# Router products by channel quarter, top-2 ranks from the logits, and five banks for the last expert's additions

## The reference, cut to what matters

```python
def moe_swiglu(h, w_router, e_gate, e_up, e_down):
    probs = jax.nn.softmax(jnp.einsum('btd,de->bte', h, w_router).astype(jnp.float32), axis=-1)
    top_v, top_i = lax.top_k(probs, TOP_K)
    top_v = top_v / jnp.sum(top_v, -1, keepdims=True)
    combine = jnp.sum(jax.nn.one_hot(top_i, N_EXPERTS, dtype=jnp.float32) * top_v[..., None], axis=-2)
    y = jnp.zeros_like(h)
    for e in range(N_EXPERTS):
        y = y + combine[..., e:e + 1].astype(h.dtype) * swiglu(h, e_gate[e], e_up[e], e_down[e])
    return y
```

## Time and profile before

| | |
|---|---|
| time, median of 3 runs | 1687.37 us (1682.82 to 1691.30) |
| the profiled execution | 1686.86 us, its span 1685.1 us |
| busy: PE, PEld | 1566.8 us (93%), 1343.1 us (80%) |
| busy: DVE, ACT, POOL | 1183.6 us (70%), 902.6 us (54%), 41.1 us (2%) |
| from HBM | 406.75 MB, 245 GB/s over the span |
| issued weight loads of the experts | 268 of 1024 KB |

### The profile page before, as it was taken

One profiled execution on the slowest core, in us unless ns is written; L12 is line 12 of the kernel. 1 busy time (PEld: TensorE's weight loads), 2 busy tenths in 40 slices (PEclk: granted clock), 3 DMA queues, 4 the chain that ended last, 5 costly groups with the idle time before them and its releaser, 6 DMA issues.

```text
span 1685.1 us, 23549 instructions
## 1 busy us (share of the span) xinstructions
PE 1566.8 (93%) x9218; PEld 1343.1 (80%) x9218; DVE 1183.6 (70%) x1232; ACT 902.6 (54%) x822; POOL 41.1 (2%) x76
## 2 busy tenths in 40 slices
PE   6999988799999799886799999999999999999995
PEld 3778777699999699775778888888888888888873
DVE  2332447755556865666598988889788888988875
ACT  2544423433333456242377767677676766767653
POOL 2100010000000010000000000000000000000000
PEclk9899978999999899878699999999999999999997
DMA  9999844254444252231299999999999999999990
GB/s 315 326 338 313 281 139 127 80 158 150 149 148 146 75 171 99 60 107 51 75 326 361 359 309 354 335 363 350 309 358 339 364 340 319 357 341 365 331 333 32
DMA packets 242035, 415.10 MB, mean 246 GB/s; under 512 B 7891, under 2 KB 128893, under 8 KB 241926
## 3 DMA queue, kind: packets, MB, share of 16 engines
q1 hardware_dynamic: 238662, 402.31, 69.7%
q0 software_dynamic: 3264, 11.28, 2.3%
HBM read 406.75 MB, written 6.82 MB: 245 GB/s over the span
## 4 chain that ended last, share of the span: by engine, by line
PE 54%; DVE 4%; ACT 1%; issue 1%; DVEq 0%; ACTq 0%
PE bank L608 15%; PE bank L610 15%; PE bank L609 15%; PE bank L1035 1%; PE bank L997 1%; PE bank L611 1%; PE bank L612 1%; PE bank L613 1%; PE bank L1077 1%; PE bank L712 1%; PE bank L727 1%; PE bank L1078 1%; PE bank L952 1%; PE bank L731 0%; PE bank L963 0%
## 5 line engine op out<-in xcount | busy, mean ns | idle before, releaser
L1496 DVE TENSOR_TENSOR w_lo<-raw_ring,w_hi 128x2048 fp32r<-128x2048 f32 x264 | 604.5, 2291 | 110.9 <-ACT w_hi L1234 110.1
L1234 ACT ACTIVATE w_hi<-raw_ring 128x2048 fp32r<-128x2048 f32 x264 | 506.7, 1919 | 238.5 <-PE bank L610 238.5
L608 PE MATMUL bank<-w_hi,xg_hi 128*128 128x512 f32 (+1 forms) x768 | 294.1, 383 | 5.4 <-DVE xg_lo L1986 5.4
L610 PE MATMUL bank<-w_hi,xg_lo 128*128 128x512 f32 (+1 forms) x768 | 289.8, 377 | 0.0
L609 PE MATMUL bank<-w_lo,xg_hi 128*128 128x512 f32 (+1 forms) x768 | 289.5, 377 | 0.0
L611 PE MATMUL bank<-act_hi,w_hi 128*128 128x320 f32 x736 | 240.4, 327 | 33.2 <-DVE act_lo L1546 20.3
L612 PE MATMUL bank<-act_lo,w_hi 128*128 128x320 f32 x736 | 234.7, 319 | 0.0
L613 PE MATMUL bank<-act_hi,w_lo 128*128 128x320 f32 x736 | 234.3, 318 | 0.0
L1487 DVE TENSOR_TENSOR w_lo<-raw_ring,w_hi 128x2048 fp32r<-128x2048 f32 x65 | 148.7, 2288 | 103.0 <-ACT w_hi L1174 102.8
L611 PEld LDWEIGHTS bank<-act_hi,w_hi 128*128 128x128 f32 x736 | 145.6, 198 | 39.3 <-issue 30.6
L608 PEld LDWEIGHTS bank<-w_hi,xg_hi 128*128 128x128 f32 x768 | 145.2, 189 | 30.5 <-DVE xg_lo L1986 5.6
(11 more groups left out here) (311 smaller groups left out, 2000.7 us busy)
## 6 DMA issues: line engine op xcount, KB each, us to landing
raw_ring<-in_e_gate_dram SPq DMA_DIRECT2D x90, 1024.0 KB, 5.2
raw_ring<-in_e_up_dram SPq DMA_DIRECT2D x90, 1024.0 KB, 5.3
raw_ring<-in_e_down_dram SPq DMA_DIRECT2D x88, 1024.0 KB, 5.0
raw_ring<-in_w_ada_dram SPq DMA_DIRECT2D x24, 1024.0 KB, 7.7
raw_ring<-in_w_in_dram SPq DMA_DIRECT2D x24, 1024.0 KB, 7.6
st<-in_w_ada_dram SPq DMA_DIRECT2D x12, 1024.0 KB, 8.5
kdsp<-in_w_ada_dram SPq DMA_DIRECT2D x12, 1024.0 KB, 9.6
raw_ring<-in_w_ff_gate_dram SPq DMA_DIRECT2D x11, 1024.0 KB, 5.4
```

The source lines that it names most:

```text
L608: pe.matmul(out, xh, wh, start=start, stop=False)
L610: return pe.matmul(out, xl, wh, start=False, stop=stop)
L1234: act.activation(w_hi[:, (NSPLIT + i) % SPL, :], raw[:, s, :], ACT.Copy).then_inc(hi_ready.sem, 1)
L1496: dve.tensor_tensor(w_lo[:, r, :], raw[:, s, :], w_hi[:, r, :].bitcast(F32), ALU.subtract).then_inc(lo_ready.sem, 1)
```

## The change

- The router's products are made by channel quarter: TensorE waits for quarter a of `hf` and multiplies its two channel slices for all token tiles, then waits for the next. The three tiles' sums now stand open side by side, in banks 5, 6 and 7, and DVE copies them with three instructions.
- The comparisons that give the ranks read the logits (`lg[:, 0]`) and not the probabilities. The sum, the reciprocal and the product that make the probabilities move behind the second token turn, in front of the routing weights; ACT's Exp stays where it is.
- The position counts (`places`) stand between the third and the fourth token turn on TensorE, and DVE's work on them between the fourth and the fifth.
- The last expert's scatter goes through banks 0 to 4 in turn; only the sixth to eighth wait for a bank to be read. The other experts' scatters stay on bank 0.

```diff
--- before.py
+++ after.py
@@ -943,15 +943,30 @@
                         sums(l, 1, m)
 
 
-            pe.wait_ge(hp_ready.sem, hp_ready.at(DEPTH - 1, 7))
-            pe.wait_ge(hs_ready.sem, hs_ready.at(DEPTH - 1, 7))
             rows_of = [[(0, P, 0)], [(0, P, P)], [(0, TS, TP), (TS, P, TP)]]
-            for t in range(NT):
-                for kk in range(KD):
-                    for r0, r1, t0 in rows_of[t]:
-                        last = pe.matmul(bank[5][r0:r1, t * NE:(t + 1) * NE], hf[:, kk, t0:t0 + r1 - r0], w_rt[:, kk, :],
-                                         start=(kk == 0), stop=(kk == KD - 1))
+            for a in range(4):
+                pe.wait_ge(hp_ready.sem, hp_ready.at(DEPTH - 1, 4 + a))
+                pe.wait_ge(hs_ready.sem, hs_ready.at(DEPTH - 1, 4 + a))
+                for kk in (2 * a, 2 * a + 1):
+                    for t in range(NT):
+                        for r0, r1, t0 in rows_of[t]:
+                            last = pe.matmul(bank[5 + t][r0:r1, 0:NE], hf[:, kk, t0:t0 + r1 - r0], w_rt[:, kk, :],
+                                             start=(kk == 0), stop=(kk == KD - 1))
             last.then_inc(rt_mm.sem, 1)
+
+            def places():
+
+                pe.wait_ge(sel_ready.sem, 1)
+                for t, t0, n in VTILES:
+                    for u in range(t):
+                        pe.matmul(bank[6][:, t * NE:(t + 1) * NE], ones[:], sel[:, u, :], start=(u == 0), stop=False)
+                    for r0, r1, _ in rows_of[t]:
+                        pe.matmul(bank[6][r0:r1, t * NE:(t + 1) * NE], before[0:n, 0:r1 - r0], sel[0:n, t, :],
+                                  start=(t == 0), stop=True)
+                for t, t0, n in VTILES:
+                    last = pe.matmul(bank[6][:, NT * NE:(NT + 1) * NE], ones[0:n, :], sel[0:n, t, :],
+                                     start=(t == 0), stop=(t == NT - 1))
+                last.then_inc(pos_mm.sem, 1)
 
             i = 0
             for t in range(NT):
@@ -964,18 +979,8 @@
                                              ident[:], start=True, stop=True)
                     last.then_inc(h2_T.sem, 1)
                     i += 1
-
-            pe.wait_ge(sel_ready.sem, 1)
...
-            last.then_inc(pos_mm.sem, 1)
+                    if i == 3:
+                        places()
 
             pe.wait_ge(h2_lo.sem, 2 * NT)
 
@@ -1065,17 +1070,20 @@
 
             def scatter(rd, e, m):
 
+                b = bank[m % 5 if e == NE - 1 else 0]
                 if m == 0:
                     pe.wait_ge(GT_read.sem, GT_read.at(rd, e))
                     pe.wait_ge(wsl_ready.sem, wsl_ready.at(rd, e))
                     if e % 2 and e < NE - 1:
                         pe.wait_ge(xg_lo_ready.sem, xg_lo_ready.at(rd, NF * (e + 1) // 2 + NF - 1))
-                else:
-                    pe.wait_ge(sc_read.sem, sc_read.at(rd, KD * e + m - 1))
+                elif e < NE - 1 or m >= 5:
+                    pe.wait_ge(sc_read.sem, sc_read.at(rd, KD * e + m - (1 if e < NE - 1 else 5)))
+                if m == 1 and e == NE - 1:
+                    pe.wait_ge(ea_ready.sem, ea_ready.at(rd, NE * NEB - 1))
                 if m % 4 == 0:
                     pe.wait_ge(yw_lo.sem, yw_lo.at(rd, 2 * e + m // 4))
-                pe.matmul(bank[0][:, 0:T], y_hi[:, m * P:(m + 1) * P], GT[:], start=True, stop=False)
-                pe.matmul(bank[0][:, 0:T], y_lo[:, m * P:(m + 1) * P], GT[:], start=False, stop=True).then_inc(sc_mm.sem, 1)
+                pe.matmul(b[:, 0:T], y_hi[:, m * P:(m + 1) * P], GT[:], start=True, stop=False)
+                pe.matmul(b[:, 0:T], y_lo[:, m * P:(m + 1) * P], GT[:], start=False, stop=True).then_inc(sc_mm.sem, 1)
 
             def experts(rd):
 
@@ -1928,17 +1936,15 @@
 
 
             dve.wait_ge(rt_mm.sem, 1)
-            link(dve.tensor_copy(lg[:, 0], bank[5][:, 0:NT * NE].rearrange("p (t e) -> p t e", e=NE)))
+            for t in range(NT):
+                last = dve.tensor_copy(lg[:, 0, t, :], bank[5 + t][:, 0:NE])
+            link(last)
             over_e = lambda r: red[:, r, :].unsqueeze(2).to_broadcast([P, NT, NE])
             link(dve.tensor_reduce(red[:, 0, :], lg[:, 0], AX.X, ALU.max))
             dve.tensor_tensor(lg[:, 1], lg[:, 0], over_e(0), ALU.subtract).then_inc(rt_sub.sem, 1)
-            dve.wait_ge(rt_exp.sem, 1)
-            link(dve.tensor_reduce(red[:, 1, :], lg[:, 1], AX.X, ALU.add))
-            link(dve.reciprocal(red[:, 2, :], red[:, 1, :]))
-            link(dve.tensor_tensor(lg[:, 1], lg[:, 1], over_e(2), ALU.mult))
             for t in range(NT):
-                mine = lg[:, 1, t, :].unsqueeze(2).to_broadcast([P, NE, NE])
-                other = lg[:, 1, t, :].unsqueeze(1).to_broadcast([P, NE, NE])
+                mine = lg[:, 0, t, :].unsqueeze(2).to_broadcast([P, NE, NE])
+                other = lg[:, 0, t, :].unsqueeze(1).to_broadcast([P, NE, NE])
                 dve.tensor_tensor(cmp[:, 0, t], other, mine, ALU.is_gt)
                 last = dve.tensor_tensor(cmp[:, 1, t], other, mine, ALU.is_equal)
             link(last)
@@ -1956,21 +1962,25 @@
                     ins = dve.tensor_tensor(tok_hi[TS:P, t, cols], bank[1 + i % 4][TS:P, :], tok_hi[TS:P, t, cols].bitcast(F32),
                                             ALU.subtract)
                 ins.then_inc(h2_lo.sem, 1)
-                if i == 2:
+                if i == 1:
+                    dve.wait_ge(rt_exp.sem, 1)
                     dve.wait_ge(sel_ready.sem, 1)
+                    link(dve.tensor_reduce(red[:, 1, :], lg[:, 1], AX.X, ALU.add))
+                    link(dve.reciprocal(red[:, 2, :], red[:, 1, :]))
+                    link(dve.tensor_tensor(lg[:, 1], lg[:, 1], over_e(2), ALU.mult))
                     link(dve.tensor_tensor(lg[:, 4], lg[:, 1], sel, ALU.mult))
                     link(dve.tensor_reduce(red[:, 3, :], lg[:, 4], AX.X, ALU.add))
                     link(dve.reciprocal(red[:, 4, :], red[:, 3, :]))
                     link(dve.tensor_tensor(comb, lg[:, 4], over_e(4), ALU.mult))
-
-            dve.wait_ge(pos_mm.sem, 1)
...
+                if i == 3:
+                    dve.wait_ge(pos_mm.sem, 1)
+                    link(dve.tensor_reduce(cnt[:, 8:9], bank[6][:, NT * NE:(NT + 1) * NE], AX.X, ALU.max))
+                    dve.tensor_scalar(cnt[:, 9:10], cnt[:, 8:9], P + 0.5, 1.0, ALU.is_gt, ALU.add)
+                    link(dve.tensor_scalar(cnt[:, 10:11], cnt[:, 8:9], 2 * P + 0.5, None, ALU.is_gt))
+                    dve.tensor_tensor(rounds_i[:], cnt[:, 9:10], cnt[:, 10:11], ALU.add).then_inc(rounds_ready.sem, 1)
+                    link(dve.scalar_tensor_tensor(posm, bank[6][:, 0:NT * NE].rearrange("p (t e) -> p t e", e=NE), 1.0, sel,
+                                                  ALU.add, ALU.mult))
+                    link(dve.tensor_scalar(posm, posm, -1.0, None, ALU.add))
 
             def mark_slots(rd, p):
 
@@ -2020,7 +2030,7 @@
                 dve.wait_ge(sc_mm.sem, sc_mm.at(rd, KD * e + m))
                 if e:
                     dve.wait_ge(sc_read.sem, sc_read.at(rd, KD * (e - 1) + m))
-                dve.tensor_tensor(accT[:, m, :], accT[:, m, :], bank[0][:, 0:T], ALU.add).then_inc(sc_read.sem, 1)
+                dve.tensor_tensor(accT[:, m, :], accT[:, m, :], bank[m % 5 if e == NE - 1 else 0][:, 0:T], ALU.add).then_inc(sc_read.sem, 1)
 
             def experts(rd):
 
```

More of the change, by code:

```diff
@@ L966, in _ @@
                     i += 1
-            pe.wait_ge(sel_ready.sem, 1)
-            for t, t0, n in VTILES:
-                for u in range(t):
-                    pe.matmul(bank[6][:, t * NE:(t + 1) * NE], ones[:], sel[:, u, :], start=(u == 0), stop=False)
-                for r0, r1, _ in rows_of[t]:
-                    pe.matmul(bank[6][r0:r1, t * NE:(t + 1) * NE], before[0:n, 0:r1 - r0], sel[0:n, t, :],
-                              start=(t == 0), stop=True)
-            for t, t0, n in VTILES:
-                last = pe.matmul(bank[6][:, NT * NE:(NT + 1) * NE], ones[0:n, :], sel[0:n, t, :],
-                                 start=(t == 0), stop=(t == NT - 1))
-            last.then_inc(pos_mm.sem, 1)
+                    if i == 3:
+                        places()
             pe.wait_ge(h2_lo.sem, 2 * NT)
@@ L1964, in _ @@
                     link(dve.tensor_tensor(comb, lg[:, 4], over_e(4), ALU.mult))
-            dve.wait_ge(pos_mm.sem, 1)
-            link(dve.tensor_reduce(cnt[:, 8:9], bank[6][:, NT * NE:(NT + 1) * NE], AX.X, ALU.max))
-            dve.tensor_scalar(cnt[:, 9:10], cnt[:, 8:9], P + 0.5, 1.0, ALU.is_gt, ALU.add)
-            link(dve.tensor_scalar(cnt[:, 10:11], cnt[:, 8:9], 2 * P + 0.5, None, ALU.is_gt))
-            dve.tensor_tensor(rounds_i[:], cnt[:, 9:10], cnt[:, 10:11], ALU.add).then_inc(rounds_ready.sem, 1)
-            link(dve.scalar_tensor_tensor(posm, bank[6][:, 0:NT * NE].rearrange("p (t e) -> p t e", e=NE), 1.0, sel,
-                                          ALU.add, ALU.mult))
```

(3 more changed lines are left out.)

## The result

The changed kernel takes 1670.39 us (median of 5 runs, 1667.32 to 1674.55) against 1687.37 for the kernel before (5 runs, and not 3 as the table ahead has it; 1682.82 to 1691.30). The ratio of the two is 0.9908, its 95% interval 0.9887 to 0.9929. Run again later it took 1673.40 (6 runs) against 1687.51 (11 runs), ratio 0.9915 (0.9898 to 0.9932). 1675.0 had been forecast: the first median lies 1.1 us under the forecast's own range (1671.5 to 1678) and within the wider one (1670 to 1681.5), the second within both. The profiled execution took 1674.03 us, its span 1672.3.

The account below looks back on a forecast made before the run. TensorE's products bound the experts, so gains lay in the chains ahead and behind: 5.8 (first gather) + 6.6 (five banks) = 12.4 off 1686.86 gives 1674.5, median 1675.0; own range 1671.5 to 1678, wider 1670 to 1681.5.

Parts of the forecast that it names:

- The experts move as a block: Expert part: paced by TensorE's products whenever they start, so an earlier first gather moves all of it, length unchanged.
- Router by quarter: Router products: 2.20 us a quarter, last ending at 800.80 instead of 807.41; H is the end of ScalarE's last modulated quarter.
- Ranks: VectorE behind the router: `sel` ends at 804.71 against 811.36, POOL's memset beside it priced at nothing.
- Turns and counts: Token turns and position counts: three turns take 5.46 us, ending at 806.26; counts done at 808.6, last low part at 813.1.
- Loop entry: VectorE ahead of the slot marks: 1.15 us behind the last low part; first gather 6.4 earlier if they overlap, not 5.8.
- Five banks: Last expert's eight additions: 0.40 us apart on VectorE alone, gaining 6.6 us, or 5.4 at the other end.
- What I put at nothing: Norm behind the additions moves as it is at the low clock; up to 2.5 us gained if the clock stays up.
- The rival of the late clock: Turns four to six: clock not yet risen, so 5.46 us instead of 2.8, 2.7 lost, 1677.7; chance 0.22.
- The rival of the early clock: Router or gather: clock up sooner, first three turns 2.8 us instead of 5.46, time written as 1672; chance 0.10.
- put the first gather at nothing: Expert part: the weight stream paces it by itself, so the front's 5.8 us are lost, 1680.8; chance 0.05.
- keep the pairs in turn: Last additions: pairs and additions still take turns, so the end gives nothing, 1681.6; chance 0.04.
- drain at a bank change: Router products: each waits for its result at bank changes, 0.79 us instead of 0.275, time 1690.6; chance 0.04.

Follow-up runs that it names:

- v_mixed_order: Kernel before with its one wait for all of hf, but router products in the changed kernel's order, three banks and three copies; 1686.06 us, 1 run.
- p_banks: Kernel before with only the five banks for the last expert's additions; 1678.80 us, ratio 0.9961 to the kernel before.
- p_marks: Kernel before with only the position counts moved between token turns three and four; 1688.24 us, ratio 1.0013 to the kernel before.
- v_tiles_outer: Changed kernel with token tiles as the outer loop inside each quarter's router products; 1674.57 us, ratio 0.9924 to the kernel before.
- v_two_banks: Changed kernel with the last expert's additions through two banks instead of five; 1676.03 us, 1 run.
- p_router: Kernel before with only the router's products by quarter, three banks and three copies; 1680.10 us, ratio 0.9965 to the kernel before.
- v_no_marks: Changed kernel with the position counts put back behind the last token turn; 1674.59 us, 1 run.

## Why the prediction was right, step by step

- **The experts move as a block: right.** 805.0 to 805.8 us from the first product's start to the last one's in every profile, whatever lay ahead.
- **Router by quarter: mechanism right, its size off.** Forecast H + 2.25 for the last product (800.80), measured H + 3.50. The step that failed is "0.275 each and 2.20 for a quarter's eight": it carried the price of the products over to another order. Splitting the mean by form would not have saved it, since a quarter has four wide and four narrow products, 4 x 0.44 + 4 x 0.12 = 2.24. What the sum lacks is a term for going from wide to narrow and back, 0.21 us, once in the order before and twice in each quarter. In the mixed order a quarter takes 2.55 us, longer than the 2.25 between quarters, so TensorE falls behind by 0.3 a quarter. `v_mixed_order` shows it without the four waits. The prediction had named more than 2.25 for a quarter as a sign that the forecast is wrong, and this sign came true; that it cost nothing in the end was luck, as the point on the turns tells.
- **Ranks: timing right, worth nothing.** From the first copy to the end of `sel` 3.14 were forecast; 804.09 to 807.03 is 2.94. TensorE reached the counts 1.0 us after it. GpSimd's memset, at 803.52 to 805.75 in the changed kernel, lay over this chain and cost nothing visible: the comparisons are 0.14 apart as before. The Trainium skill's rule (GPSIMD Engine Reference, section Specifications), by which such instructions contend with GpSimd, allowed 0.7 us; the trace shows none.
- **Turns and counts: right in sum, by luck.** Three turns took 4.25 instead of 5.46, the clock having risen earlier within them. These 1.2 us, which the sum did not have, cancel the 1.25 of the late router. The last low part ended at H + 14.45, forecast H + 14.55.
- **Loop entry: the value taken was wrong, its bound right.** I took 1.15 and kept a gain of 0.6 as a bound; it was 0.19, a gain of 0.96. Before, VectorE's load of the number of rounds waits for its own last compute instruction (L1973, done at 818.88) and starts at 818.91; with the counts early it waits for none of the low parts, starts at 813.93 and runs under the last one (until 814.86). From the load's start to the slot marks it is 1.12 us in both. This is almost the whole difference between 5.8 forecast and 6.85 measured. Where the counts stand last it is 1.15 in every profile.
- **Five banks: right.** 6.6 forecast, 6.61 measured in the whole. In `p_banks` the time fell by 6.6 us (3.9 to 9.3). Against the other profiles with one bank it would be 6.9, by the clock.
- **What I put at nothing** brought 0.49 at the gather and 0.66 in the norm, both by the clock: part of the gather, and L719, now run while it is still up. Of the 0.66, 0.3 to 0.4 is only the late fall of the clock in this profile of before.
- **The rival of the late clock** had the right place and another mechanism. In all six profiles with the counts between turns three and four the clock was up while the counts ran (it had risen 1.3 us ahead of them at the earliest, and in `p_marks` and `v_tiles_outer` within 0.2 us of their start), and in four it fell again behind them. Priced at 2.7, it costs 2.15 in `v_two_banks`, of which 1.6 by the fall. The changed kernel's two profiles are those that escaped it.
- **The rival of the early clock** has a small slip: `sel` at 804.71 and the end of the third turn at 806.26 are 1.55 apart, and not 1.7. Nothing else uses it.
- **The clock under the router's products: as the trace of before had it.** 10.19 us of unbroken TensorE work at a granted 0.50. The Trainium skill's rule (TensorE: Matmul & The Clock Gate, section What's actually happening), that activity of the engine releases the half rate, does not describe these; it does fit the turns: the clock rose within the first three or just at their end in every profile.
- **The rivals that put the first gather at nothing, keep the pairs in turn, or drain at a bank change** are each refuted: `p_router` gains in time what its front gains (5.9 and 6.0 us), the additions stand 0.40 apart, and the last product ended at H + 3.50.

So the gain is router products (6.0) plus banks (6.6 to 6.9), and what ranks and counts add to the front lies between a gain of 0.8 and a loss of 1.3 by the draw of the clock: `v_no_marks` at 16.79 and `p_router` at 16.83 are the same. Whether that draw is what makes one kernel's runs differ by 7 us is open; the stretches that I compared differ by far less between profiles, and the work ahead of H, which the change doesn't touch, by up to 5.3 (796.88 to 802.14).

## What to carry to other kernels

Before a row's mean is used for work in another order, split it by form and count how often the forms alternate in either order: here both forms' prices gave the same sum as the mean, and the alternation was what it left out (0.21 us each time). Short matmuls of few columns can fill TensorE's row in the profile and the granted clock fall all the same: here it did behind 2.2 us of them in four profiles of six, and cost 1.6 us of the dense work that followed. With the counts behind the last turn no such work waits, and the front was 16.79 both times. Where pairs of producer and consumer alternate through one buffer at the very end of a chain, a second buffer brings most of the gain (5.6 of 6.6 us here).

## What the runs showed of the hardware

- Narrow products (64 stationary columns, 8 moving) cost 0.12 us each in a run of sixteen at the granted clock 0.50, and in pairs among wide ones about 0.20 (10.19 us for eight groups of two wide at 0.44 and two narrow). Each going from wide to narrow and back costs 0.21 us (8.74, 9.36 and 10.19 us for one, four and eight of them: the kernel before, `v_tiles_outer`, the changed kernel).
- A change of PSUM bank between wide products of the router costs nothing (records 0.213 us apart with it and without), nor does one between pairs of the last additions (0.15).
- Behind the 2.2 us of position counts between the third and the fourth turn the granted clock fell from 1.00 to 0.50 in four of six profiles (in `v_two_banks` within 0.5 us of their end), though TensorE was busy throughout.
- A matmul pair and VectorE's addition that take turns through one bank need 1.14 us a round at the full clock (additions at 1642.43, 1643.56 and 1644.70 before) and 1.48 at the half clock; through two banks 0.57, through five 0.40, which is VectorE alone.
